# First shift and scale by blocks of 128 features inside the first map, and a reordered opening of the attention mixer

## The reference, cut to what matters

```
mod_lat = (silu_c @ w_ada[l] + b_ada[l])        # 1024 x 6144 weights: six vectors of 1024
mod_ctx = silu_cc @ w_ada[l] + b_ada[l]
sh1, sc1, gt1, sh2, sc2, gt2 = split(mod_lat, 6)
h  = rms_norm(x, g_mix[l])   * (1 + sc1)  + sh1     # 512 positions
hc = rms_norm(ctx, g_mix[l]) * (1 + csc1) + csh1    # 256 positions
f_in, c_q, c_kv, k_rope = split(h @ w_in[l])        # 256, 384, 128, 32 columns
q = rms_norm(c_q) @ w_q_b ; kv = rms_norm(c_kv) @ w_kv_b     # 12 heads, 64 + 32 wide
four = fft2(f_in).real @ w_fourier + b_fourier
mix = concat([four, softmax(q k^T) v]) @ w_out
```

## Time and profile before

| what | value |
|---|---|
| runs | 3166.83 us median (3166.53 to 3167.48) |
| profiled execution, its own time | 3169.61 us |
| its span | 3167.8 us |
| PE busy | 3083.2 us, 97% |
| DVE, ACT, POOL busy | 1554.6, 1174.6, 160.8 us |
| mean DMA rate | 89 GB/s, 297 GB/s in the first fortieth of the span |

### The profile page before, as it was taken

The page is one execution under the profiler, slowest core; times in us unless marked ns, Lnnn a source line. Parts: engine busy times, 40 slices in busy tenths (PEclk is TensorE's granted clock), DMA queues, the critical chain, the costliest instruction groups (busy, mean ns, idle before and its releaser), DMA issues.

```text
span 3167.8 us, 43261 instructions
## 1 busy us (share of the span) xinstructions
PE 3083.2 (97%) x17758; PEld 2489.5 (79%) x17758; DVE 1554.6 (49%) x2356; ACT 1174.6 (37%) x1921; POOL 160.8 (5%) x222
## 2 busy tenths in 40 slices
PE   7989899999999999999999999999999999999999
PEld 4767787887888867888888777888888777788887
DVE  3245555434445455564546653355433677544445
ACT  3144533213223345442435632343222445432333
POOL 0022200000000012100000010000000013000000
PEclk9999999999999999999999999999999999999999
DMA  7521124333112221223232211122222221223222
GB/s 297 193 48 36 38 62 158 140 122 124 61 60 74 97 56 45 67 87 95 91 100 90 81 35 41 47 94 93 93 94 93 80 78 41 88 93 104 96 93 73
DMA packets 81283, 281.92 MB, mean 89 GB/s; under 512 B 11064, under 2 KB 11576, under 8 KB 80320
## 3 DMA queue, kind: packets, MB, share of 16 engines
q1 hardware_dynamic: 81088, 279.16, 27.1%
HBM read 261.29 MB, written 2.10 MB: 83 GB/s over the span
## 4 chain that ended last, share of the span: by engine, by line
PE 93%; DVE 3%; ACT 1%; issue 1%; DMA 1%; SPq 0%; POOL 0%; POOLq 0%; ACTq 0%; DVEq 0%
PE PS L534 67%; PE PS L1868 3%; PE PS L497 3%; PE PS L1783 2%; PE PS L1892 2%; PE PS L1879 2%; PE PS L671 1%; PE PS L518 1%; PE PS L3583 1%; DMA room<-in_w_ada 1%; DVE room L2109 1%; PE PS L3048 1%; PE PS L1813 0%; PE PS L2367 0%; PE PS L3038 0%
## 5 line engine op out<-in xcount | busy, mean ns | idle before, releaser
L534 PE MATMUL PS<-room,WHI 128*128 128x512 f32 x6776 | 1921.9, 375 | 8.5 <-DVE H L2254 2.0
L534 PEld LDWEIGHTS PS<-room,WHI 128*128 128x128 f32 x6776 | 1188.5, 188 | 273.9 <-issue 38.0
L534 PE MATMUL PS<-room,WLO 128*128 128x512 f32 (+1 forms) x3388 | 1159.5, 372 | 0.0
L534 PEld LDWEIGHTS PS<-room,WLO 128*128 128x128 f32 x3388 | 595.3, 188 | 113.9 <-issue 1.0
L358 ACT ACTIVATE WHI<-RING 128x1024 fp32r<-128x1024 f32 x369 | 388.1, 1054 | 568.3 <-PE PS L534 491.0
L367 DVE TENSOR_TENSOR WLO<-RING,WHI 128x1024 fp32r<-128x1024 f32 x369 | 452.1, 1225 | 196.0 <-ACT WHI L358 194.7
L1344 DVE SCALAR_TENSOR_TENSOR H<-PS,VEC,H 128x511 f32<-128x511 f32 (+1 forms) x132 | 83.1, 657 | 298.0 <-ACT H L1322 297.9
L1322 ACT ACTIVATE H<-PS,VEC 128x512 f32<-128x512 f32 (+1 forms) x132 | 88.5, 704 | 338.7 <-PE PS L534 336.1
L1265 DVE SCALAR_TENSOR_TENSOR X<-PS,MOD,X 128x512 f32<-128x512 f32 x91 | 57.5, 659 | 205.2 <-PE PS L534 205.2
L2109 DVE TENSOR_REDUCE room<-PS 128x1 f32<-128x768 f32 (+1 forms) x120 | 101.6, 847 | 62.8 <-PE PS L1868 62.5
L3630 DVE TENSOR_TENSOR room<-PS,room 128x512 f32<-128x512 f32 x64 | 44.2, 690 | 157.6 <-ACT room L3626 102.5
(11 more groups left out here) (418 smaller groups left out, 3045.3 us busy)
## 6 DMA issues: line engine op xcount, KB each, us to landing
RING<-in_stream SPq DMA_DIRECT2D x370, 512.0 KB, 3.5
room<-in_w_ada SPq DMA_DIRECT2D x84, 512.0 KB, 5.4
H<-in_w_ada SPq DMA_DIRECT2D x12, 512.0 KB, 3.9
room<-in_wq SPq DMA_DIRECT2D x2, 1728.0 KB, 7.2
room<-room SPq DMA_DIRECT2D x18, 192.0 KB, 2.6
X<-in_x_in SPq DMA_DIRECT2D x2, 1536.0 KB, 10.1
WLO<-WLO SPq DMA_DIRECT2D x12, 192.0 KB, 2.6
room<-in_wple SPq DMA_DIRECT2D x2, 1024.0 KB, 4.8
```

The costliest lines, as they stand in the source:

```text
L534: mm = pe.matmul(acc, wt[:, w], xt[:, k * xw + lo:k * xw + lo + q], start=(k == ks[0] and z == 0), stop=(k == ks[-1] and z == 2))
```

## The change

`AdaBlocks` replaces the first `AdaSet`. A block is 128 features of shift and scale: all 1024 input rows, 256 columns, loaded by two DMAs whose rows are 512 bytes long. It has 8 matmuls of 256 columns, one copy, two small matmuls against `SEL` that also sum over the four groups of partitions, and its own bias and gain. The first block is made in `begin`, the second in `normalize`, block k+2 inside the first map at tile k.

```
+class AdaBlocks:
+    def fetch(self, sp, t):
+        if t >= ADA_STEPS:
+            sp.wait_ge(*self.summed.at(t - ADA_STEPS + 1))
+        slot = self.slot(t).rearrange("p (k g n) -> p k g n", k=KT, g=2)
+        for g in range(2):
+            src = self.source[g * KT:(g + 1) * KT].rearrange("k p n -> p k n")[:, :, t * P:(t + 1) * P]
+            sp.dma_start(slot[:, :, g, :], src).then_inc(*self.landed[t].up())
...
 linear:
                 for j in range(group):
                     products(j, k, range(2))
+                if middle is not None:
+                    middle(pe, k)
                 pe.wait_ge(*ready(k))
                 for j in range(group):
                     products(j, k, range(2, 3))
...
 in_proj:
-           supply=supply, slots=2 if l == 0 else MIXED, ahead=False)
+           supply=supply, slots=2 if l == 0 else MIXED, ahead=False,
+           middle=lambda pe, k: blocks.step(pe, k + 2) if blocks is not None and k + 2 < KT else None,
+           weave=lambda pe, k: blocks.turn(pe, k + 2) if blocks is not None and k + 2 < KT else None)
...
 normalize, scalar:
+        if blocks is not None:
+            split_hi(c, act, 2)
+            blocks.copy(act, 1)
...
+            if blocks is not None and 1 <= k < nk - 1:
+                blocks.copy(act, k + 1)
 normalize, vector:
         def scale(k):
+            if blocks is not None:
+                blocks.add(dve, k)
...
         scale(0)
+        if blocks is not None:
+            split_lo(c, dve, 2)
 begin, sync:
+        blocks.fetch(sp, 0)
+        fetch(c, sp, args, SLOTS)
+        for k in range(1, 4):
+            blocks.fetch(sp, k)
+        fetch(c, sp, args, SLOTS + 1)
+        for k in range(4, KT):
+            blocks.fetch(sp, k)
+        fetch(c, sp, args, SLOTS + 2)
...
 mix_heads:
-    query_order = (0, 4, 1, 2, 5, 3) if l == 0 else range(tiles_q)
+    query_order = lambda p: (0, 4, 1, 2, 5, 3) if l == 0 and p < 5 else range(tiles_q)
...
+        move_q(0)
         move_k(0)
         place_key(0)
-        move_q(0)
         place_rope(0)
...
-        for kind in "KWSLQ":
+        for kind in "QKWSL":
             head(kind, 0)
```

More of the change, by code:

```diff
@@ L1155, in root_of, with normalize @@
     return c.bank(6, n) if lo == 0 else c.bank(7, n)
-def normalize(c, squares, gain, xp, shift=None, keep=None, prep=None, over=None, keep_spread=None, gap=4):
+def normalize(c, squares, gain, xp, shift=None, keep=None, prep=None, over=None, keep_spread=None, gap=4, blocks=None):
     n, nk = squares.n, squares.nk
@@ L1169, in normalize, with _ @@
     place = keep or (lambda k, a, m: c.ht(k % 3, a, m))
+    if blocks is not None:
+        @block.tensor
+        def _(pe):
+            for t in range(2):
+                if t:
+                    blocks.step(pe, t)
+                blocks.turn(pe, t)
     @block.scalar
     def _(act):
+        if blocks is not None:
+            split_hi(c, act, 2)
+            blocks.copy(act, 1)
         for k in range(nk):
@@ L1206, in normalize, with modulated @@
     return Tiles(hi, lo)
-def modulated(c, l, g, part, squares, xp, made, last=None, free=None):
-    gains = c.mark("dve", 2)
+def modulated(c, l, g, part, squares, xp, made, last=None, free=None, blocks=None):
+    gains = c.mark("dve", 2) if blocks is None else None
     def prep(dve):
@@ L1532, in apply, with in_proj @@
             ins.then_inc(*self.done.up())
-def in_proj(c, args, l, ready, xp, sets, qnorm, knorm):
+def in_proj(c, args, l, ready, xp, sets, qnorm, knorm, blocks):
     pr = A1["PROJ"]
@@ L1844, in _ @@
             mm.then_inc(*placed.up())
[L1845 to L1853, removed]
+        for k in range(2):
+            pe.wait_ge(*ft_out.at(k + 1))
+            for q in range(2):
+                if k == 0:
+                    own((2 * q, 2 * q + 1), four.at(q + 1))
+                for r, (lo, n, *_) in enumerate(spans):
+                    mm = pe.matmul(c.bank(2 * q + r, n), c.a(A1["WF"] + k * FW + q * P, P), ft(k, lo, n), start=(k == 0), stop=(k == 1))
+                if k == 1:
+                    mm.then_inc(*mixed.up())
         def score(a, b):
@@ L1887, in values @@
             if i in (0, 4):
-                own((6 + part,), o_out.at(parts * pair + parts - part))
+                nth = part if pair == 5 else parts - 1 - part
+                own((6 + part,), o_out.at(parts * pair + nth + 1))
             n, t0 = steps[a][3], steps[a][2] // P
@@ L1949, in in_order @@
             ins.then_inc(*ft_out.up())
[L1950 to L1955, removed]
+        for kind in "RQKS":
+            head(kind, 0)
+        for q in range(2):
+            in_order(q)
         for q in range(2):
             act.wait_ge(*mixed.at(q + 1))
-            act.activation(c.h(q, 0, nq), c.PS[:, 1024 * (1 + q):1024 * (1 + q) + nq], ACT.Identity,
+            act.activation(c.h(q, 0, nq), c.PS[:, 1024 * q:1024 * q + nq], ACT.Identity,
                            bias=c.vec(f"b_four{l}", q)).then_inc(*four.up())
@@ L3292, in block1 @@
                 if l == 0:
-                    ready = modulated(c, l, f"g_mix{l}", 0, squares, xp, sets[0].done.at(2))
+                    ready = modulated(c, l, f"g_mix{l}", 0, squares, xp, None, blocks=blocks)
                 else:
@@ L3322, in begin @@
     ring = [(room[:, 2 * j * UN:(2 * j + 1) * UN], room[:, (2 * j + 1) * UN:(2 * j + 2) * UN]) for j in range(ADA_STEPS)]
-    sets = [AdaSet(c, args, ring, rows, 0, s, (0, 4, 5)[s], [(8 * s + k) % ADA_STEPS for k in range(KT)]) for s in range(3)]
-    c.emptied = [ada.summed.at(k + 1) for ada in sets[:1] for k in range(KT)]
+    blocks = AdaBlocks(c, args, room, rows, "g_mix0")
+    sets = [AdaSet(c, args, ring, rows, 0, s, (0, 4, 5)[s], [(8 * s + k) % ADA_STEPS for k in range(KT)]) for s in (1, 2)]
+    c.emptied = [blocks.summed.at(k + 1) for k in range(KT)]
     loaded, silu = c.mark("dma", 2), c.mark("act")
     x_loaded = [c.mark("dma") for _ in range(2)]
-    zero, ones = c.mark("dve"), c.mark("dve", 4)
+    zero, ones, picked = c.mark("dve"), c.mark("dve", 4), c.mark("dve")
     block = c.stage()
@@ L3376, in _ @@
         pe.wait_ge(*ones.at(4))
[L3377 to L3382, removed]
+        pe.wait_ge(*picked.at(1))
+        blocks.step(pe, 0)
+        squares.sums(pe)
+    return blocks, sets
 FINAL_ORDER = (5, 6, 7, 0, 1, 2, 3, 4)
```

90 lines of the change are left out of this document (66 added, 24 removed).

## The result

The changed kernel takes 3180.22 us, the median of 5 runs (3178.11 to 3181.98), against 3166.83 of the kernel before (5 runs, 3165.39 to 3167.48): a ratio of 1.0042, 95% interval [1.0027, 1.0057]. 3152.4 was predicted, so 27.8 us are missing, and the sign is wrong: a loss of 8.6 to 18.1 us where a gain was forecast. The profiled execution took 3180.22, its span is 3178.4 us.

What follows compares the result with a forecast made beforehand. PE was taken to bound the kernel, with 93% of the chain. Gains of 2.5 + 5.2 + 2.4 + 4.3 = 14.4 us took the median from 3166.83 to 3152.4 us; own range 3143 to 3158, overall 3142 to 3166.

Steps and rivals of the forecast that it cites:

- Behind each place PE is the chain, so what is gained there is kept: Whole kernel: the four gains add up to 14.4 us off the time, with nothing lost behind them.
- The opening: Start to first two units: loading w_ada in blocks starts the first map earlier; 2.5 us gained, bound above 5.5.
- the small work: Opening, before the map: PE's totals, idle products and spread after the first block, reckoned from durations in the earlier profile.
- The rounds: Inside the first map: DVE's loop sets the pace, one tile per 3.95 us.
- The step: Opening: a block's matmuls on PE, taken as half of 1.93 us, and 0.45 us per step inside the map.
- the loop eats the opening: Rival, first map: DVE's waits or half clock make rounds 4.5 to 5.5 us; total 3155 to 3159.5; chance 0.10.
- Slow blocks: Rival, opening: 512-byte rows load at half the rate, 6.9 us a block; total 3172.2; chance 0.08.
- The mixer's opening, layer 0: Before layer 0's first score: Q ahead removes PE's wait and keeps the clock up; 5.2 us gained, bounds 2.7 and 6.2.
- Layer 1: Mixer's opening in layer 1: Q leaves ahead of K, 1.8 us idle left; 2.4 us gained, bounds 1 and 6.4.
- End of the attention: Layer 0, last score to next map: context tiles last shorten the tail; 4.3 us gained, bounds 0 and 6.5.
- The three mixer terms: The gains put for layer 0's mixer opening (5.2), layer 1 (2.4) and the attention's end (4.3).
- Rival 3: Mixer: transfers end as late, clock falls, tail keeps its length; only 6.2 us gained in all, 3160.6; chance 0.10.

Runs made afterwards that it cites:

- warm_opening3: Changed kernel with SEL in EPSC's free columns (old places), plus 49 unread PE products ahead of the first block and 6 before the map: 3150.31 us, ratio 0.9955.
- blocks_only: Kernel before with only the opening's blocks added, SEL in EPSC's free columns (old places), mixer as before: 3169.88 us, ratio 1.0013.
- mixer_only: Kernel before with only the mixer's part: Q ahead of K, W and transform, last pair's context tiles last; opening and places unchanged: 3151.44 us, ratio 0.9953.
- mixer_near64: Kernel before with the mixer's part alone, and AV's 64 bytes put ahead of the rounded weights, so rooms lie 64 bytes nearer to them: 3139.92 us, ratio 0.9914.
- warm_opening2: Changed kernel with SEL in EPSC's free columns (old places), plus 40 unread PE products ahead of the first block and 6 before the map: 3154.55 us, ratio 0.9957.
- both_mended: warm_opening3 with AV's 64 bytes put ahead of the rounded weights: 3136.37 us, ratio 0.9901.

## Why the prediction was wrong

1. *The step that failed*: "Behind each place PE is the chain, so what is gained there is kept." PE was the chain, but the sum took for granted that all that the diff does not move keeps its duration. The diff's first line, a tile of two columns, moved every room by 32 bytes against the weights, and each large matmul behind layer 0 took 4.4 ns more. By ratios that is 1.0042 less 0.9974, 0.68% or 21.5 us. This term was not in the sum and no rival named it. Without it the change gains 8.2 us (5.7 to 11.1).

2. *The opening*, "2.5 us gained": the second step that failed. The durations of totals, spread and idle products (1.48, 1.50, 1.95) came from one execution in which PE did this work at full clock; in six of ten executions of the old opening the totals take 2.65 and 2.56 instead, and the new opening had these in all four traces where PE stood idle ahead of the first block. The sum had put nothing for that: the small work took 11.8 us where 7.2 were reckoned, and 6.9 once PE came to it without a gap (warm_opening3). The sum had taken 0.9 off for the clock at the map's start alone. The rounds, 4.25 instead of 3.95, add 1.8 us (six of them; the low products take 0.97, not 0.72). The step was halved by mistake, as said above: 0.97 and 0.45 were put, and at full clock it takes 1.00; inside the map DVE's loop covers most of that. Together: the first units were to end at 60.4 and ended at 67.91, and at 61.60 in warm_opening3. Against the trace of before the opening lost 5.0, just past the end of the rival "the loop eats the opening" (0 to -4.6), whose mechanism is only a part of it; over the whole run blocks_only lost 1.3 to 7.0.

3. *Slow blocks* did not come: 290 GB/s against the 304 of the straight line (and the 408 of rows of 4 KB), and no wait for `w_ada` inside the map.

4. *The mixer's opening, layer 0*, was right, mechanism and size: the first score came 2.9 us earlier (2.75 predicted), without idle time and at clock 1.00, and between 117 and 198 us the changed kernel and mixer_only both gained 5.0 on the kernel before, where 5.2 had been put.

5. *Layer 1*: 2.4 predicted with bounds 1 and 6.4, "the upper if the 4 us of half clock go too". They went: the wait is 1.22, where 1.8 was said, and between 1097 and 1147 us the lead grows by 5.4 in the changed kernel and 5.1 in mixer_only.

6. *End of the attention*: 4.3 predicted, with 6.2 us between last score and map; 6.31 came, and the lead over the trace of before grows by 5.0 (mixer_only) to 6.7 (the changed kernel) up to 400 us. That this is near is in part luck: the 12.33 that the sum started from is 1.6 longer than in six other executions of the old order, which themselves gain 2.7 to 2.8 at this place. Against those the new order gains some 2 to 4 us.

7. The three mixer terms were 11.9 together and the part alone measured 14.9 (9.8 to 19.6, so the two agree). Rival 3 ("the mixer's gains don't come") is false.

What stays open: why just these distances are good or bad (0 and +256 bytes are alike, which a period of 256 would explain, but no run shows the mechanism; at -64 the first room begins 166 x 256 bytes behind WHI, and one such place is no more than a hint), and why layer 0 answers the other way.

## What to carry to other kernels

Before adding a tile, look at what it moves: put it behind the big tiles or into free columns, and when a stretch that the change does not touch takes longer, count its matmuls in equal windows before looking for a wait. A duration read from a row holds for the clock at which that row ran, and for that execution: ask what PE did just before, and look at the same row in a second execution before a sum rests on it. And where matmuls are most of the time, it is worth trying a few distances between the streaming tiles and the weights: here 64 bytes were worth 11.5 us (mixer_only against mixer_near64).

## What was not expected of the hardware

- The pace of 128x512 matmuls depends on the distance in SBUF between the input and the weights: 226.7, 228.9, 232.4 or 233.3 ns, in the same maps and at a granted clock of 1.00 in these windows.
- The granted clock's column reads 1.00 ahead of the trace's first record of the clock (29.01 us in the changed kernel, 42.89 in mixer_only) while the work runs at half speed: 21 and 20 matmuls in 20 to 28 us with 1.00 in one kernel and with 0.50 in another. There durations tell more than the column.
- The same products ahead of the first block helped or not by what PE did right behind them: where it then waited for the block until 17.85 the totals ran at 0.50 (2.65 us, warm_opening2), where it went on without a wait they took 1.43 (warm_opening3, both_mended). No wait is no warrant: in both_mended PE came to totals and idle products without a wait too, and the clock fell to 0.50 at 21.2 us all the same.
